# A PEER layer's gathered tiles: four experts of 32 tokens instead of one expert of 128, summed in four column strips

## The reference, cut to what matters

```python
s = jnp.einsum("thsd,hskd->thsk", q, p["peer_keys"])      # two halves of 128 keys
s_top, i_top = lax.top_k(s, 16)
cand = s_top[:, :, 0, :, None] + s_top[:, :, 1, None, :]  # 16 x 16 candidates
g_score, c_idx = lax.top_k(cand, 16)
experts = e1 * 128 + e2
gates = jax.nn.softmax(g_score, axis=-1)
u = jnp.take(p["peer_u"], experts, axis=0)
act = jax.nn.gelu(jnp.einsum("thkd,td->thk", u, hb), approximate=False) * gates
v = jnp.take(p["peer_v"], experts, axis=0)
return jnp.einsum("thk,thkd->td", act, v)
```

## Time and profile before

| | |
|---|---|
| median of 3 runs | 4652.68 us (4650.27 to 4655.88) |
| the profiled execution | 4654.25 us |
| its span on the core | 4652.2 us |
| mean granted clock of TensorE | 0.936 of full |
| PE, DVE, POOL, ACT busy | 3932.5, 2817.1, 1545.6, 1133.9 us |
| gathers | 1280, from 819.78 and from 3282.55 us |
| all DMA | 1488.24 MB |

### The profile page before, as it was taken

The page is one execution under the profiler, slowest core; times in us unless marked ns, Lnnn a source line. Parts: engine busy times, 40 slices in busy tenths (PEclk is TensorE's granted clock), DMA queues, the critical chain, the costliest instruction groups (busy, mean ns, idle before and its releaser), DMA issues. The chain is left out here.

```text
span 4652.2 us, 37588 instructions
## 1 busy us (share of the span) xinstructions
PE 3932.5 (85%) x12086; PEld 2013.1 (43%) x12086; DVE 2817.1 (61%) x6867; ACT 1133.9 (24%) x2935; POOL 1545.6 (33%) x1383
## 2 busy tenths in 40 slices
PE   7998989788888788788788887799888898877777
PEld 4646755444443343333333333487544443333333
DVE  1513654677777777765555553743778888555554
ACT  2111222222222222221222211354322323111111
POOL 0001310344444444445444441000244344444443
PEclk9998989899998998889999998999999999999999
DMA  4102641999999999999999995100699999999998
GB/s 162 55 19 89 230 162 40 387 414 409 413 415 399 405 399 407 404 395 421 421 420 417 422 416 224 36 1 21 270 419 420 414 410 411 422 421 422 422 422 338
DMA packets 229365, 1488.24 MB, mean 320 GB/s; under 512 B 25760, under 2 KB 31264, under 8 KB 58928
## 3 DMA queue, kind: packets, MB, share of 16 engines
q0 software_dynamic: 184320, 1342.26, 70.1%
q1 hardware_dynamic: 43472, 139.52, 8.4%
q10 hardware_dynamic: 1376, 4.06, 0.2%
HBM read 1483.61 MB, written 2.13 MB: 319 GB/s over the span
## 5 line engine op out<-in xcount | busy, mean ns | idle before, releaser
L1550 PE MATMUL banks<-arena 128*128 128x512 f32 x5120 | 2441.5, 634 | 593.3 <-ACT arena L1675 554.0
L1433 POOL DMA_INDIRECT arena<-experts,arena x1280 | 1472.7, 1151 | 2513.0 <-PE banks L1550 1761.2
L1787 DVE CUSTOM_DVE_ANT_0 arena<-arena 128x1024 f32<-128x1024 f32 x1280 | 1544.7, 1224 | 936.1 <-DMA arena<-experts,arena 933.3
L1550 PEld LDWEIGHTS banks<-arena 128*128 128x128 f32 x5120 | 1018.5, 203 | 1959.4 <-issue 1241.0
L1675 ACT ACTIVATE arena<-arena 128x128 f32<-128x128 f32 x1280 | 407.9, 389 | 283.3 <-DVE arena L1799 268.0
L1668 ACT ACTIVATE arena<-arena 128x4 f32<-128x4 f32 x320 | 66.0, 206 | 1664.7 <-DVE arena L1787 1664.5
L1477 PE MATMUL banks<-arena 128*128 128x128 f32 (+2 forms) x1280 | 292.1, 383 | 2.1 <-DMA arena<-wq 2.1
L1477 PEld LDWEIGHTS banks<-arena 128*128 128x128 f32 x1280 | 206.6, 194 | 83.4 <-issue 15.8
L391 PE MATMUL banks<-arena 128*128 128x512 f32 (+1 forms) x640 | 210.3, 489 | 2.2 <-PEq L200 2.2
L732 POOL TENSOR_TENSOR arena<-arena 128x256 f32<-128x256 f32 x48 | 30.5, 636 | 506.7 <-ACT arena L629 376.8
L1447 PE MATMUL banks<-arena 128*128 128x512 f32 x416 | 183.0, 597 | 2.9 <-PEq L826 1.5
(11 more groups left out here) (214 smaller groups left out, 3070.5 us busy)
## 6 DMA issues: line engine op xcount, KB each, us to landing
arena<-l_w_ada SPq DMA_DIRECT2D x48, 1024.0 KB, 5.0
arena<-wq SPq DMA_DIRECT2D x80, 512.0 KB
arena<-experts,arena POOLq DMA_INDIRECT x1280
arena<-l_w_in SPq DMA_DIRECT2D x7, 2048.0 KB, 7.7
arena<-l_w_out SPq DMA_DIRECT2D x4, 1536.0 KB, 12.3
arena<-keys SPq DMA_DIRECT2D x40, 128.0 KB
arena<-l_w_o SPq DMA_DIRECT2D x4, 1024.0 KB, 8.5
arena<-gates SPq DMA_DIRECT2D x6, 512.0 KB, 6.2
```

The source lines that it names most:

```text
L1433: pool.indirect_dma_start(slots[u % NS], None, tbl, bass.IndirectOffsetOnAxis(ap=expert[:, c % RING, k:k + 1], axis=0)).then_inc(land[u % ...
L1550: mm = pe.matmul(core["ps"][:, c, :], diag[:, k % (2 * BATCH), :], v[:, D + c * 512:D + (c + 1) * 512], start=(i % PH == 0 and k == 0), st ...
L1787: dve.tensor_tensor_reduce(u, u, h2[:, i // PH, :], 1.0, 0.0, ALU.mult, ALU.add, dots[:, k:k + 1]).then_inc(dot["sem"], up(dot))
```

## The change

A buffer holds the same 128 rows of 8 KB, but they are now four experts of 32 tokens: gather 4s + j fetches, for tokens 32j to 32j+31 of the tile, the experts 4s to 4s+3, expert 4s + r in partitions 32r to 32r+31. The number and the bytes of the gathers are the same.

- **Weighted sum.** The weights are 32 columns: a matrix of four stacked 32x32 identities times the weights of the rows. Its product with a buffer sums four experts and gives 32 tokens, which go to partitions 32j to 32j+31 of the banks. The halves c are now the outer loop, so the buffers of a batch are freed in the second half.
- **Choice.** After `choose_b` (both results now in `xg`) PE spreads expert numbers and gates to the new layout with 16 products with parts of the identity (`spread_choice`), and DVE copies them out (`choice_out`), a batch later in the main loop. POOL waits for that copy.
- **Gates.** DVE multiplies the stacked identities with the gates of a whole position at once (`gate_identity`, 128x512). ACT scales 32 columns of it by the gelu into the diagonals. `weigh` is gone.
- **Token rows.** The u half must meet the row of token 32j + n in each partition 32r + n. PE multiplies 32 columns of `ht` with the identity into four strips (`spread_rows`, 32 products per j), ACT copies 128x1024 out (`rows_spread`). For tile 0 all four j stand in the preamble at t = 1; for the later tiles they stand behind batches 1 to 4 of the tile before (`REP_AT`). `turn_back` and `rows_back` are gone.
- **Memory.** 10 buffers in each layer; 6 instead of 8 may start early in layer 1. The second row of gates `g2` is fetched when it is needed. Scratch areas move; `PREP_AT` starts at 132.

```diff
-    "slots": [RO + n * ROWS for n in range(6)] + [L0] +
-     [L0 + 9216 + n * ROWS for n in range(4)]},
+    "rep": (L0 + 3072, L0 + 7168), "ht": HO,
+     "slots": [RO + n * ROWS for n in range(6)] + [L0] + [L0 + 11264 + n * ROWS for n in range(3)]},
...
-     "slots": [HO + n * ROWS for n in range(8)] + [RO + SLOT + n * ROWS for n in range(4)]},
+     "slots": [HO + n * ROWS for n in range(6)] + [RO + SLOT + n * ROWS for n in range(4)]},
...
-            def turn_back(t):
...
+            def spread_rows(t, j):
+                n = 4 * t + j
+                pe.wait_ge(ncl["sem"], at(ncl, tiles if t else 1))
+                pe.wait_ge(nch["sem"], at(nch, tiles if t else 1))
+                if n:
+                    pe.wait_ge(rpo["sem"], at(rpo, n))
+                q = slice(t * P + 32 * j, t * P + 32 * j + 32)
                 for k in range(KD):
+                    for r in range(4):
+                        i = pe.matmul(pair(core, 4)[32 * r:32 * r + 32, k * P:(k + 1) * P], ht[:, k, q],
+                                      ident(core), start=True, stop=True)
+                i.then_inc(rpt["sem"], up(rpt))
+
+            def spread_choice(c):
+                pe.wait_ge(xgr["sem"], at(xgr, c + 1))
+                if c >= 2:
+                    pe.wait_ge(gtd["sem"], at(gtd, c - 1))
+                for j in range(4):
+                    for r in range(4):
+                        i = pe.matmul(core["ps"][32 * r:32 * r + 32, 6 + c % 2, 8 * j:8 * j + 8],
+                                      ident(core)[:, 32 * j:32 * j + 32],
+                                      xg[:, c % 2, :].rearrange("p (n r) -> p r n", r=4)[:, r, :],
+                                      start=True, stop=True)
+                i.then_inc(pmt["sem"], up(pmt))
...
-                    turn_back(t - 1)
+                if t == 1:
+                    for j in range(4):
+                        spread_rows(0, j)
+                if 2 <= t < tiles:
+                    spread_choice(t - 2)
...
+                for c in range(2):
+                    for j in range(BATCH):
+                        v = slots[(g * BATCH + j) % NS]
+                        mm = pe.matmul(core["ps"][32 * j:32 * j + 32, c, :], diag[:, g % 2, j, :],
                                        v[:, D + c * 512:D + (c + 1) * 512],
+                                       start=(g % (NB * PH) == 0), stop=(g % (NB * PH) == NB * PH - 1))
+                        if c == 1:
+                            mm.then_inc(free["sem"], up(free))
+                if half_at(g) and half_at(g)[1] == 1:
+                    spread_choice(half_at(g)[0])
+                if g % (NB * PH) in REP_AT and g // (NB * PH) + 1 < tiles:
+                    spread_rows(g // (NB * PH) + 1, REP_AT.index(g % (NB * PH)))
...
+                act.wait_ge(gid["sem"], at(gid, i + 1))
+                act.wait_ge(gl["sem"], at(gl, g + 1))
+                for j in range(BATCH):
+                    ins = act.activation(diag[:, g % 2, j, :], gated[:, i % 2, b * BATCH + j, :], ACT.Copy,
+                                         scale=gel[:, b * BATCH + j:b * BATCH + j + 1])
...
+            def choice_out(c):
+                r = c % RING
+                got = core["ps"][:, 6 + c % 2, 0:32].rearrange("p (j n) -> p j n", j=4)
+                dve.wait_ge(pmt["sem"], at(pmt, c + 1))
+                dve.tensor_copy(expert[:, r, :].rearrange("p (s j) -> p j s", j=4),
+                                got[:, :, 0:4]).then_inc(rdy["sem"], up(rdy))
...
             for g in range(POS):
                 dot_batch(g)
+                if half_at(g - 1) and half_at(g - 1)[1] == 1:
+                    choice_out(half_at(g - 1)[0])
+                if g % NB == NB - 1 and g + 1 < POS:
+                    gate_identity(g // NB + 1)
...
-                weigh(g)
```

More of the change, by code:

```diff
@@ L1245, in peer_block @@
     x = view(core, XO, TT, D)
-    h2 = view(core, m["h2"], tiles, D)
+    rep = [view(core, o, 4, D) for o in m["rep"]]
+    xn = view(core, m["rep"][1], 2, D)
     ht = view(core, m["ht"], KD, tiles * P)
@@ L1250, in peer_block @@
     g1 = view(core, m["g1"], conds, D)
-    g2 = view(core, m["g2"], conds, D)
-    diag = view(core, m["diag"], 2 * BATCH, P)
+    g2 = view(core, m["g2"], D)
+    diag = view(core, m["diag"], 2, BATCH, 32)
+    gated = view(core, m["diag"] + 2 * P, 2, TOPK, 32)
+    ident4 = view(core, S_ID4, 32)
     wq = view(core, m["wq"], 2, KD, SIDE)
@@ L1281, in peer_block @@
     gel = take(TOPK)
-    wts = take(TOPK)
-    assert top[0] <= MISC + 1344
+    xg = take(2, 2 * TOPK)
+    assert top[0] <= MISC + 1600
     rest = view(core, C_TRI, 2, PK)
@@ L1385, in _ @@
             load_keys(1)
-            for n in range(conds):
-                sp.dma_start(g2[:, n, :], gate_rows(core, layer, 1, n)).then_inc(gr["sem"], up(gr, 16))
+            sp.dma_start(g2, gate_rows(core, layer, 1, 0)).then_inc(gr["sem"], up(gr, 16))
             if layer == 0:
@@ L1407, in _ @@
                 sp.wait_ge(qmm["sem"], at(qmm, 2 * E))
+                sp.wait_ge(rpt["sem"], at(rpt, 4 * tiles))
                 sp.dma_start(down, d["l1_w_dqkv"].rearrange("(k p) n -> p k n", p=P)
                              ).then_inc(dwl["sem"], up(dwl, 16))
+                sp.wait_ge(rd["sem"], at(rd, TL))
+                sp.dma_start(g2, gate_rows(core, layer, 1, 1)).then_inc(gr["sem"], up(gr, 16))
                 sp.wait_ge(free["sem"], at(free, steps * TOPK))
@@ L1427, in _ @@
                     if u < NS:
-                        pool.wait_ge(omm["sem"], at(omm, 2 * tiles if layer == 0 or u >= 8 else 0))
+                        pool.wait_ge(omm["sem"], at(omm, 2 * tiles if layer == 0 or u >= 6 else 0))
                         if layer == 0:
@@ L1505, in prepare @@
                         pe.wait_ge(dwl["sem"], at(dwl, 32))
-                        pe.wait_ge(nbo["sem"], at(nbo, tiles))
+                        pe.wait_ge(gtd["sem"], at(gtd, steps))
                     else:
@@ L1570, in squares @@
                 act.wait_ge(oad["sem"], at(oad, 2 * t + 2))
-                act.activation(h2[:, t, :], x[:, t, :], ACT.Square,
+                if t >= 2:
+                    act.wait_ge(ntr["sem"], at(ntr, t - 1))
+                act.activation(xn[:, t % 2, :], x[:, t, :], ACT.Square,
                                accum_out=ss[:, t:t + 1]).then_inc(nsq["sem"], up(nsq))
@@ L1605, in scores_out, with rows_spread @@
                                ACT.Copy).then_inc(sev["sem"], up(sev))
+            def rows_spread(t, j):
+                act.wait_ge(rpt["sem"], at(rpt, 4 * t + j + 1))
+                act.activation(rep[t % 2][:, j, :], pair(core, 4), ACT.Copy).then_inc(rpo["sem"], up(rpo))
             def softmax(c):
@@ L1615, in prepare @@
                         act.wait_ge(ptr["sem"], at(ptr, u))
-                    act.activation(h2[:, 0, :], x[:, u, :], ACT.Square,
+                    act.activation(xp, x[:, u, :], ACT.Square,
                                    accum_out=ss1[:, u:u + 1]).then_inc(psq["sem"], up(psq))
@@ L1663, in _ @@
                     softmax(t - 2)
+                if t == 1:
+                    for j in range(4):
+                        rows_spread(0, j)
             for g in range(POS):
@@ L1672, in _ @@
                     act.wait_ge(free["sem"], at(free, BATCH * (g - 1)))
-                act.wait_ge(wt["sem"], at(wt, g + 1))
-                for k in range(b * BATCH, (b + 1) * BATCH):
-                    ins = act.activation(diag[:, k % (2 * BATCH), :], ident(core), ACT.Copy, scale=wts[:, k:k + 1])
+                act.wait_ge(gid["sem"], at(gid, i + 1))
[3 more added lines that the diff above has]
+                                         scale=gel[:, b * BATCH + j:b * BATCH + j + 1])
                 ins.then_inc(dg["sem"], up(dg))
+                if (g - 1) % (NB * PH) in REP_AT and (g - 1) // (NB * PH) + 1 < tiles:
+                    rows_spread((g - 1) // (NB * PH) + 1, REP_AT.index((g - 1) % (NB * PH)))
                 if g - 3 in event_at:
```

115 lines of the change are left out of this document (56 added, 59 removed).

## The result

The changed kernel takes **4725.24 us** (4719.45 to 4725.41) beside 4652.16 of the kernel before: ratio **1.0153**, 95% interval 1.0135 to 1.0171, about 73 us slower. The forecast was 4640, so both its sign and its range were wrong.

The account below looks back on a forecast made before the run. The prediction took the DMA rate of the gathers as the bound, a fixed 3190 us; its terms, 28 + 0 + 1 - 3 - 32 - 7 = -13 us against the median of 4652.68, gave about 4640 us, range 4612 to 4682.

Parts of the forecast that it names:

- The bound: In both PEER stages the DMA rate of 420 to 422 GB/s is the ceiling, a fixed 3190 us for 1280 gathers.
- Part 1, the sum: TensorE's weighted sum in strips takes 2 us, about 4 at the lower clock, so 5 to 6 us shorter.
- Part 3, fewer buffers: Gather stages with 10 buffers: quicker returns outweigh lost cover in layer 0, -32 us, and come out even in layer 1, 0.
- The spot of rows 4: A starved batch in layer 0's gathers, where POOL idled 10.39 us; buffers were to return 2 to 6 us sooner.
- The bounds of the recovery: Of the 51 us lost inside the gather stretches, the change recovers between nothing and all.
- Rival A: Gather stages: the shorter ring starves as before, buffers returning sooner only by the cover lost; recovery 0, 4672 us, 28%.
- Part 2: Weighing leaves DVE, so PE no longer waits for DVE in batches with a choice's second half; costed at nothing.
- Parts 4 and 5: Ahead of the gathers: repeated first-tile rows, +28 us for both layers; spreading choices instead of turning back, 0, layer 1 +1.
- Parts 6 and 7: Layer 1's first sum about 7 us sooner, -3 us net; the ends after each layer's last tile, together -7 us.
- Rival B: Gather stages and preambles: all ring loss is recovered and the strips are at their floor, 4615 us, 15%.
- D: Rival on TensorE: strips don't overlap, each sum stays 6.87 us and each turn 7.1, 4715 us, 5%.

Follow-up runs that it names:

- ring-of-before run: The changed kernel with 11 buffers in layer 0 and 12 in layer 1, repeated rows of all tiles but the first left out: 4630.71 us, ratio 0.9959.

## Why the prediction was wrong, point by point

- *The bound.* Right: the pure stretches stayed within 3 GB/s of before (418 and 419 by the stretch), and TensorE's share fell to 57% without a gain.
- *Part 1, the sum.* Right in its length: 3.64 us at the low clock, 1.92 at the high one, beside "2 to 4". The saving was less than the "5 to 6 us" said: in the mean of the 320 sums it is 7.6 us before (2441.5 / 320) and 3.3 after (1043.1 / 320), 4.4 us.
- *Part 3, fewer buffers.* **This is the step that failed.** It took -32 us in layer 0 and 0 in layer 1. Measured from first gather to last dot product, layer 0 lost 35.4 us and layer 1 25.2. Two mistakes made it. The first was in the estimate of the returns. The spot of rows 4 was said to free all four at 1971.5 to 1973, that is 10.4 to 11.9 us after the last dot product began; the trace of after shows the gathers issued 12.1 to 16.9 after it. The softmax's wait (7.0 us from the last dot product's start), the diagonals (0.9), a sum at the low clock that frees nothing in its first half, and POOL's own 1.25 to 1.75 us per gather all add up, and I had counted POOL's not at all. The returns at this spot are 0.3 to 1.9 us sooner, not 2 to 6; over all batches of layer 0 the mean is 1.4 us for the first gather and 2.4 for the fourth, no more than the 2.49 taken away. The second was the bound. "The bounds of the recovery are nothing and all" left out a loss, although I had worked out that 2.5 and 5.0 us of cover were being taken away. The runs show 84 to 87 us for those buffers, one in layer 0 and two in layer 1.
- *Rival A* was the right mechanism with its price cut off at the same bound: it stood at 4672, since it let the loss stay as it was rather than grow. Its deciding point, returns sooner by 2.49 us or less, is what the trace shows in the mean and in the batches with a first half; its reason was only half of it, since the sum did run at the low clock, but the unchanged wait for the softmax is what kept the buffers.
- *Part 2* said in passing that in batches with a first half the diagonals still wait 5.6 us. It was costed at nothing because both kernels have it. But the same wait costs more when the ring is shorter: with it moved away in both, the changed kernel is 8 us behind instead of 73. That wait was most of what made buffers scarce.
- *Parts 4 and 5.* Close: 11.4 us per layer against 14.2, a spread 0.37 against 1.2. Layer 0's first gather came 10.3 us later, 14 had been said. The Trainium skill's page TensorEngine Tiling (Array Packing), "Instruction Overhead", gave an estimated 0.8 us for the spread. The measured 0.37 us, at a granted clock of 1.00, is under half of that, so the page's figure is too high for these instructions and the 1.2 us was further off still.
- *Parts 6 and 7.* Right in kind. Layer 1's first sum started 39.7 us after its first gather (3372.36 - 3332.63) instead of 48.7, 9 sooner where 7 was said. From the last dot product's start (4711.61) to the end of the span it is 11.9 us instead of 15.9, the 4 us said.
- *Rival B* (all recovered) and *D* (strips in turn) did not come. At the old ring, the rate of 416 of the ring-of-before run shows that most of what B supposed was within reach.

## What to carry to other kernels

Where a queue of transfers is the bound and a ring of buffers feeds it, cost a change in two terms: how many buffers it takes, and how much sooner the last step gives one back, measured from the same event to the next issue, with every wait of an in-order engine on that chain; a matmul a third as long behind an unchanged 7 us wait returned buffers 0.4 to 1.7 us sooner. A short ring's price is not linear (in the changed layout 84 us for the cut to ten buffers, 165 for the one to nine), so the bounds of such a term must take in a loss. And look on that chain for calls that wait for work which nothing behind them needs: moving one softmax took 87 us off the changed kernel, and with the weighing moved too it took 22 off the kernel before.

## What the runs showed of the hardware that was not expected

Filler products raised the granted clock from 0.745 to 0.843 and made the kernel 27 us slower; the buffers of layer 0 came back 0.5 us later in the mean (8.5 instead of 8.0 us to a batch's first gather).

While gathers run, long strings of small matmuls don't always flow. The same 64 instructions that take 1.95 us in the preamble took 4.4 in one place of the run with the softmax moved: the first 47 flowed, and the other 17 came in groups of 4 and 5, some 0.73 us apart:

```profile
1909.28 1.49 PE L1485 MATMUL banks<-arena 128*32 128x128 f32 x47
1911.00 0.42 PE L1485 MATMUL banks<-arena 128*32 128x128 f32 x4 [0.23 <-issue]
1911.74 0.41 PE L1485 MATMUL banks<-arena 128*32 128x128 f32 x4 [0.32 <-issue]
1912.47 0.44 PE L1485 MATMUL banks<-arena 128*32 128x128 f32 x5 [0.31 <-issue]
1913.20 0.43 PE L1485 MATMUL banks<-arena 128*32 128x128 f32 x4 [0.29 <-issue]
```

The engine waited for nothing that the profile shows. Other strings beside gathers did flow, in 1.92 and 1.96 us (1958.57 and 1968.95 us in the changed kernel's timeline). The cause was not looked for.
